# The MLP of a decoder step by one level of Strassen's algorithm, in two phases

## What is computed

```python
def out_and_mlp(x, a, b, w_out, g_mlp, w_up, w_down):
    x = x + jnp.concatenate([a, b], axis=-1) @ w_out
    hn = rmsnorm(x, g_mlp)
    return x + jnp.square(jax.nn.relu(hn @ w_up)) @ w_down
...
    y_prompt = rmsnorm(xp, g_final)
    y_sample = rmsnorm(xs, g_final)
```

## Time and profile before

| | before |
|---|---|
| median of 3 runs (1789.96 to 1799.34) | 1791.36 us |
| span of the profiled execution, first to last instruction | 1663.6 us |
| around the span, against the median | 127.8 us |
| TensorE busy | 1624.7 us, 98% |
| VectorE, ScalarE, GpSimd busy | 52%, 41%, 35% |
| mean granted TensorE clock | 0.987 |
| the MLP, first matmul to the end | 888 to 1664 us |

### The profile page before, as it was taken

One profiled execution on the slowest core, in us unless ns is written; L12 is line 12 of the kernel. 1 busy time (PEld: TensorE's weight loads), 2 busy tenths in 40 slices (PEclk: granted clock), 3 DMA queues, 4 the chain that ended last, 5 costly groups with the idle time before them and its releaser, 6 DMA issues.

```text
span 1663.6 us, 29654 instructions
## 1 busy us (share of the span) xinstructions
PE 1624.7 (98%) x11324; PEld 1395.8 (84%) x11324; DVE 857.5 (52%) x2059; ACT 686.5 (41%) x1448; POOL 587.2 (35%) x715
## 2 busy tenths in 40 slices
PE   8999999999989999999999999999999999999997
PEld 6653464699976777676899999999999999999997
DVE  5486889987644566765545323232323224232424
ACT  4574887688246655553522212122221212222223
POOL 1100333468467777773235031232305022231300
PEclk8999999999989999999999999999999999999999
DMA  8211302235589877779201020111111020111102
GB/s 252 62 51 55 116 28 79 58 90 172 188 262 319 295 248 222 253 207 277 75 1 51 18 85 1 59 43 50 50 50 50 0 101 0 50 50 50 64 2 107
DMA packets 88619, 174.34 MB, mean 105 GB/s; under 512 B 10619, under 2 KB 38639, under 8 KB 88258
## 3 DMA queue, kind: packets, MB, share of 16 engines
q1 hardware_dynamic: 67138, 101.17, 18.4%
q0 software_dynamic: 21376, 71.75, 14.0%
HBM read 152.01 MB, written 20.88 MB: 104 GB/s over the span
## 4 chain that ended last, share of the span: by engine, by line
PE 80%; DVE 7%; issue 6%; DMA 4%; ACT 1%; POOL 1%; SPq 0%; DVEq 0%; ACTq 0%; POOLq 0%
PE psum L2046 8%; PE psum L2044 8%; PE psum L2034 8%; PE psum L2032 8%; PE psum L2033 8%; PE psum L2045 8%; PE psum L1707 3%; PE psum L1827 2%; PE psum L1849 2%; PE psum L1867 2%; PE psum L1506 2%; PE psum L1969 2%; PE psum L1973 2%; PE psum L1968 2%; PE psum L1549 2%
## 5 line engine op out<-in xcount | busy, mean ns | idle before, releaser
L1373 ACT ACTIVATE hrelu<-psum 128x384 f32<-128x384 f32 (+1 forms) x96 | 45.5, 474 | 504.1 <-PE psum L2034 504.1
L2032 PE MATMUL psum<-n_hi,wup_hi 128*128 128x384 f32 (+1 forms) x768 | 251.0, 327 | 0.0
L2044 PE MATMUL psum<-h_hi,wdn_hi 128*128 128x384 f32 (+1 forms) x768 | 250.9, 327 | 0.0
L2034 PE MATMUL psum<-n_hi,wup_lo 128*128 128x384 f32 (+1 forms) x768 | 250.8, 327 | 0.0
L2033 PE MATMUL psum<-n_lo,wup_hi 128*128 128x384 f32 (+1 forms) x768 | 250.8, 327 | 0.0
L2046 PE MATMUL psum<-h_hi,wdn_lo 128*128 128x384 f32 (+1 forms) x768 | 250.2, 326 | 0.0
L2045 PE MATMUL psum<-h_lo,wdn_hi 128*128 128x384 f32 (+1 forms) x768 | 250.0, 326 | 0.0
L2699 DVE TENSOR_TENSOR h_lo<-h_full,h_hi 128x384 fp32r<-128x384 f32 (+1 forms) x96 | 115.7, 1219 | 257.8 <-ACT h_hi L1381 249.0
L2704 DVE TENSOR_TENSOR x_region<-psum,x_region 128x384 f32<-128x384 f32 (+1 forms) x192 | 102.9, 536 | 252.8 <-PE psum L2046 251.7
L1044 POOL TENSOR_TENSOR wup_lo<-wup_full,wup_hi 128x4096 fp32r<-128x4096 f32 x8 | 72.5, 9064 | 384.6 <-ACT wup_hi L1349 384.6
L1220 ACT ACTIVATE arena<-x_region,arena 128x384 bf16<-128x384 f32 (+2 forms) x192 | 166.5, 872 | 6.4 <-POOL arena L969 6.3
(11 more groups left out here) (349 smaller groups left out, 3118.4 us busy)
## 6 DMA issues: line engine op xcount, KB each, us to landing
wup_full<-in_w_up SPq DMA_DIRECT2D x8, 2048.0 KB, 7.7
wdn_full<-in_w_down SPq DMA_DIRECT2D x8, 2048.0 KB, 7.9
arena<-k_scratch SPq DMA_DIRECT2D x32, 256.0 KB
arena<-in_x_prompt SPq DMA_DIRECT2D x14, 512.0 KB, 11.4
arena<-in_w_in SPq DMA_DIRECT2D x3, 2048.0 KB
arena<-in_w_in SPq DMA_DIRECT2D x12, 512.0 KB, 6.0
k_scratch<-arena SPq DMA_DIRECT2D x24, 256.0 KB, 2.6
out<-arena SPq DMA_DIRECT2D x17, 256.0 KB, 3.4
```

The costliest lines, as they stand in the source:

```text
L2032: pe.matmul(b, wu_hi[:, k, col], n_hi[:, k, o:o + w], start=(k == 0), stop=False)
L2034: i = pe.matmul(b, wu_lo[:, k, col], n_hi[:, k, o:o + w], start=False, stop=(k == KT - 1))
L2044: pe.matmul(b, wd_hi[:, f, col], h_hi[:, hf, 0:w], start=(f == 0), stop=False)
```

## The change

The prompt's MLP runs by Strassen's algorithm in Winograd's form: each matrix product is cut in quarters, and seven products of half size stand for eight, with sums before and behind. It has two phases.

Up: 16 groups of 256 hidden features. The activation quarters and their sums (`n`, `xT` used as a buffer, `t4`) are made once, by token blocks of 64 (even and odd blocks are the two halves). Per group SP loads raw w_up (1 MB), GpSimd makes four sums of 512 columns, ScalarE seven high parts, VectorE seven low parts; TensorE runs seven products of 12 matmuls (512 token columns; in group 0 in two passes of 384 and 128). Products 3, 5 and 6 accumulate onto banks that hold 0, 2 and 4. ScalarE and VectorE combine and square them to h, VectorE makes four sums, and SP stores seven tiles of 256 KB to `hscr`. GpSimd also makes the four sums of w_down, through DRAM (`sscr`). x goes to `xscr` before the phase and comes back in the next one.

Down: 112 steps (product i, group k) of 12 matmuls of 512 columns in four banks. Each step's operands (2 x 256 KB) come into a ring of six slots; ScalarE makes the high part (1024 columns), VectorE the low part.

The sample tokens are stationary operands of 64 columns: per up group 48 matmuls with 128 moving columns, in 4 of 7 down products 3 matmuls of 512 a step. The final norm turns all second halves and the sample tile during the last product, and the first halves of the eight prompt tiles behind it.

The diff, cut to its core (i is a product, v a pass, g a group):

```diff
+VG = [(0, 0, 6), (0, 6, 8)] + [(g, 0, 8) for g in range(1, NG)]
+UPBANK = [(0, 1, 2, 0, 3, 2, 3), (4, 5, 6, 4, 1, 6, 1)]
+CHAINED = (3, 5, 6)
+DN_SAMPLE = {0: "h1", 1: "h2", 4: "hd", 5: "h1"}
+RING = 6
+ROWS_EARLY = [(t, 1) for t in range(NB)] + [(NB, 1), (NB, 0)]
...
@@ SP
+            for c in range(3):
+                park(c)
             sp.wait_ge(wo_ready, 3 * KT)
-            sp.dma_start(wd_full, w_dn_v[:, 0:4, :]).then_inc(wdn_in, 16)
...
+            raw_up(1)
+            raw_down(0)
+            sums_down(0)
+            for g in range(NG):
+                v = LASTV[g]
+                if g:
+                    raw_down(g)
+                    h_late(v - 1, g - 1)
+                    if g + 1 < NG:
+                        sp.wait_ge(w_low, 7 * g + 7)
+                        raw_up(g + 1)
+                    sums_down(g)
+                h_early(v, g)
+                if g == NG - 1:
+                    sp.wait_ge(us_done, 2 * NG - 1)
+                    fill(1)
+                    sp.wait_ge(up_done, 7 * LASTV[NG - 1] + 5)
+                    fill(2)
+                h_sums(v, g)
+            sp.wait_ge(us_done, 2 * NG)
+            fill(3)
...
@@ GpSimd
+            for g in range(NG):
+                down_sums(g)
+                if g + 1 < NG:
+                    for x in (1, 2, 3, 4):
+                        up_sum(g + 1, x)
@@ ScalarE
+            squares(0, 0, KT)
+            token_root(0)
+            squares(1, 0, 4)
+            for i in range(7):
+                up_high(0, i)
+            squares(1, 4, 5)
+            norm_high(0)
+            squares(1, 5, KT)
+            token_root(1)
+            squares(2, 0, 3)
+            norm_high(1)
+            squares(2, 3, 4)
+            t4_high(0)
+            t4_high(1)
+            squares(2, 4, KT)
+            token_root(2)
+            norm_high(2)
+            t4_high(2)
...
+            for v, (g, lo, hi) in enumerate(VG):
+                end = v == LASTV[g]
+                if g:
+                    up_high(g, 3)
+                first_product(v)
+                if g:
+                    for i in (4, 5, 6):
+                        up_high(g, i)
+                h_from_bank(v)
+                if end and g + 1 < NG:
+                    up_high(g + 1, 0)
+                    up_high(g + 1, 1)
+                h_from_tile(v, h22, 1)
...
+            for s in range(3, DN_STEPS):
+                dn_high_part(s)
+                if s == 3:
+                    hs_high_part(0, 30)
...
+            for t in range(NB):
+                y_square(len(ROWS_EARLY) + t)
+                y_root(t)
+                act.wait_ge(row_scaled, ROW_SCALED0 + t + 1)
+                act.wait_ge(g_scaled, G_SCALED0 + t + 1)
+                act.activation(yrow[t][:, 512:1024], yrow[t][:, 512:1024], ACT.Copy, scale=yroot[:, t:t + 1]).then_inc(y_rows, 1)
@@ TensorE
-                if u == KT + 3:
+                if u == KT + 1:
                     rms(0)
-                if u == 2 * KT + 3:
+                if u == 2 * KT + 1:
                     rms(1)
...
+            def up_product(v, i):
+                pe.wait_ge(w_low, 7 * g + i + 1)
+                if v == 0:
+                    pe.wait_ge(n_low, {0: 2, 2: 2, 4: 2, 5: 2}.get(i, 4))
...
+                if i == 3:
+                    pe.wait_ge(up_act, v + 1)
+                if i == 5:
+                    pe.wait_ge(up_dve, 5 * v + 2)
+                if i == 6:
+                    pe.wait_ge(up_dve, 5 * v + 3)
+                for k in range(4):
+                    first = k == 0 and i not in CHAINED
+                    pe.matmul(out, wu_hi[i][:, k, :], b_side(i, k, 0, lo, hi), start=first, stop=False, skip_group_check=True)
+                    pe.matmul(out, wu_hi[i][:, k, :], b_side(i, k, 1, lo, hi), start=False, stop=False, skip_group_check=True)
+                    ins = pe.matmul(out, wu_lo[i][:, k, :], b_side(i, k, 0, lo, hi), start=False, stop=(k == 3), skip_group_check=True)
...
+            for v, (g, lo, hi) in enumerate(VG):
+                end = v == LASTV[g]
+                up_product(v, 0)
+                if g:
+                    turn_sample_h(g - 1)
+                up_product(v, 1)
+                if v == 0:
+                    rms(2)
+                up_product(v, 2)
+                if end:
+                    up_sample(g, 0)
+                for i in (3, 4, 5, 6):
+                    up_product(v, i)
+                if end:
+                    up_sample(g, 1)
...
+            def dn_product(s):
+                pe.wait_ge(dn_low, DN_LOW0 + s + 1)
...
+                    if s < NG:
+                        pe.wait_ge(hs_low, HS_LOW0 + (1 if k < 15 else 2))
...
@@ VectorE
                 dve.tensor_tensor(xT[:, j, o:o + w], bank(u % 6)[:, 0:w], xT[:, j, o:o + w], ALU.add).then_inc(wo_done, 1)
+                if u == KT + 1:
+                    norm(0)
                 if u == KT + 4:
-                    rms(0)
+                    low_early(0)
+                if u == KT + 5:
+                    for n in range(7):
+                        up_low(0, n)
+                if u == 2 * KT + 1:
+                    norm(1)
                 if u == 2 * KT + 4:
-                    rms(1)
-            rms(2)
+                    low_early(1)
+                    norm_t4(0)
+                    norm_t4(1)
+                if u == 2 * KT + 5:
+                    low_late(0)
+                    low_late(1)
+            norm(2)
+            norm_t4(2)
+            low_last()
...
+                if g:
+                    up_low(g, 3)
+                if v:
+                    last_h_sum(v - 1)
+                dve.wait_ge(up_act, v + 1)
+                add_bank(v, 0, 1, u, u)
+                if g:
+                    keep_sample_h(g - 1)
+                    for i in (4, 5, 6):
+                        up_low(g, i)
...
+                add_bank(v, 1, 2, h22, u)
+                if end and g + 1 < NG:
+                    up_low(g + 1, 0)
+                add_bank(v, 2, 4, h22, h22)
+                if end and g + 1 < NG:
+                    up_low(g + 1, 1)
+                    up_low(g + 1, 2)
...
+                add_bank(v, 3, 5, h12, u)
...
+                add_bank(v, 4, 6, u, u)
+                dve.wait_ge(h_made, H_MADE0 + 4 * v + 3)
+                h_sum(v, 0, t3_, h22, h12, ALU.subtract)
...
```

More of the change, by code:

```diff
@@ L1070, in _, with squares @@
         def _(act):
-            def rms(c):
+            def squares(c, lo, hi):
                 o, w = CH[c]
-                for k in range(KT):
+                for k in range(lo, hi):
                     n = 8 * c + k
```

801 lines of the change are left out of this document (598 added, 203 removed).

## The result

| | before | changed |
|---|---|---|
| median beside each other, 4 runs of each | 1795.35 us | 1864.82 us (1851.14 to 1874.24) |
| ratio, 95% interval | | 1.040 (1.034 to 1.045) |
| the same on another chip, 9 and 4 runs | 1782.53 | 1853.86; 1.038 (1.035 to 1.041) |
| span of the profiled execution | 1663.6, a second one 1778.8 | 1861.2, a second one 1862.9 |
| mean granted TensorE clock | 0.987 and 0.973 | 0.946 and 0.948 |

A forecast was written before the change was run, and what follows sets the result against it. TensorE was taken to bound the kernel, busy 100 of 100 us in the MLP. Start 21, loop 21, phase change with clock 11.4, end 15, less 30 saved, gave +38.4 on 1791.4: 1830 us, range 1790 to 1862.

The forecast's parts named there:

- TensorE's work: TensorE's matmuls and transposes in the MLP: 736 us against 765.7, so 30 us saved.
- my lower bound of 0.067: Sample tokens' up matmuls of 128 columns: 0.067 us each by the column law; 0.088 was taken, halfway to 0.109.
- Rival 2: Narrow matmuls cost several passes, 128 columns as much as 512 (0.227 us): kernel at 1925 us; chance 0.08.
- rival 4: Matmuls of 512 columns cost 0.213 us, so gain and waits nearly cancel: 1793 us, no change; chance 0.09.
- The start: TensorE's waits from the end of w_out through group 0 of the up phase: 21 us, 15 to 26.
- The loop: Up phase, TensorE's wait before product 6 in each of 14 groups: 1.5 us each, 21 us in all.
- Rival 1: The preparation on ScalarE, VectorE and GpSimd hides after all, from w_out to group 15: 1786 or 1771 us; chance 0.10.
- Rival 3: The raw w_up loads come late, each microsecond costing 14: 1849 or 1892 us; chance 0.12.
- The change of phase: Between up and down, TensorE's wait before the first sample product: 8.4 us, 11.4 with clock allowances.
- The clock: Half granted clock behind idle TensorE: 1.5 us at the change of phase and as much at the start.
- The end: From the last add to the kernel's end, the final norm of eight tiles: 15 us more, 11 to 18.
- The signs: Prediction wrong if an up-phase group takes under 24 us, or three named TensorE waits are under half their forecast.

The follow-up runs named there:

- x4_start: The changed kernel with only the start of the up phase reordered on ScalarE and VectorE, seven low parts of the weights coming later: 1844.72 us, 1.036 of the kernel before.
- x1_lows_first: The changed kernel with VectorE making low parts 4, 5 and 6 ahead of product 1's add, in all groups but the first: 1822.13 us, 1.024 of the kernel before.
- x7_no_sums: The changed kernel with VectorE's up_low(g,0) no longer waiting for GpSimd's two sums, from group 1 on: 1816.20 us, 1.020 of the kernel before.
- x5_all: The changed kernel with four reorderings together (low parts before the first add, change of phase, start, tail): 1794.58 us, 1.006 of the kernel before.
- x6_packed: x5_all plus the edit of x7_no_sums, earlier low parts at the start, and sample tokens' high and low parts packed as one weight: 1783.70 us, 0.993.

## Why the prediction was right or wrong

**TensorE's work: right, by two errors of opposite sign.** 512 columns down cost 0.227, as worked out: six distances in 1.35 us, 0.226 each.

```profile
1700.82 0.39 PE L2433 MATMUL psum<-ring_hi 128*128 128x512 f32 x1
...
1702.18 0.39 PE L2433 MATMUL psum<-ring_hi 128*128 128x512 f32 x1
```

Up they cost 0.234 in six of seven products, 7.6 us more than the sum has (1080 matmuls). The sample products of 128 columns cost 0.060 (16 distances in 0.97 us), not 0.088:

```profile
1183.09 0.22 PE L2377 MATMUL psum<-wu_hi,n_lo 128*64 128x128 f32 x1
...
1184.06 0.44 PE L2356 MATMUL psum<-n_hi,wu_hi 128*128 128x512 f32 x1
```

That is 21 us less, and below my lower bound of 0.067: halfway between two bounds was the wrong choice. The bound from the earlier trace rows didn't apply: its operations have weights of 128 columns and these have 64. With weights of 128 columns the 84 prompt matmuls of 128 columns do cost 0.111 (forecast 0.109). The Trainium skill ("TensorE: Matmul & The Clock Gate", Back-to-back issue gap) gives 81 ns for 128 columns; the trace has 60 with 64-column weights and 111 with 128-column ones, so it agrees with neither. Rival 2 is out, since 128 columns cost far less than 512 (0.060 and 0.111 against 0.227), and so is rival 4, since the 512-column matmuls cost 0.227 to 0.234 and not 0.213.

**The start: places right, one price short.** The waits before products 1, 3, 5 and 6 of group 0 were forecast as 4.7, 12.3 and 1.7 and were 5.2, 11.5 and 2.6. rms(2), forecast as 1 us, didn't wait. rms(1) was forecast as 1.3 and waited 5.4; the w_out stage lost 7.5. The step had counted the squares' sum behind VectorE's seven low parts but with too short a queue; x4_start moved those and got 6.2 back.

**The loop: right in its chain, short by 9 us.** 2.1 us a group instead of 1.5, within its 0 to 4. SP's issue came 1.4 us later into the group than forecast, and GpSimd, which the forecast has busy until the load lands, was idle for 1.7 us before it. Rival 1, that the preparation hides, is out as the kernel stands; x1_lows_first and x7_no_sums show that most of the loop's part hides once one link is moved. Rival 3, late loads, is out too: their median is the forecast's 5.5.

**The change of phase: 14.0 instead of 8.4.** The forecast had one wait, before the sample product, and it was 3 us longer (11.4). There is a second, of 2.6 us, before the fourth bank of the first down step: that bank is released by the add of the last up product, which stands on VectorE behind `dn_low_part(1)`, as the trace shows. The prediction didn't walk through that queue.

**The clock: the step that failed.** It was put at 3 us, 1.5 each at the start and at the change of phase. The row it rested on, showed a half clock behind a stretch in which TensorE was busy for less than a third. The prediction used it for the two long waits only and took the 14 short ones as their own length. The runs showed 65 us at half clock in the MLP and 19.5 us lost in it outside the waits: 16.5 us more than the term has, the largest error of the sum and half of the 33 us by which the stages differ from it. Some 2 us more were lost this way in w_out's stage, behind the wait at rms(1), in the 4.2 us of this row (columns as in the earlier trace rows):

```profile
994.40:998.60 4.20, 4.20 (x13) 3.59 (x14) 0.00 (x0) 0.94 (x2) 0.45 (x1) 0.50 0.75 268
```

x1_lows_first and x7_no_sums confirm it as a consequence of the waits: 23 us fewer of these, and 10 to 13 us of slow matmuls went with them.

**The end: right** (16.3 for 15).

**The range.** It went by rivals and not by terms: the far ends of the start, the loop, the end and TensorE's saving (26, 56, 18 and 13) with the 11.4 of the phase add up to 1890. The measured time went 3 us past the 1862 that I gave, less than its own runs differ. The two terms that I gave no range, the clock and the change of phase, are 22 of the 33 us. The terms weren't independent either: each chain that was longer than I had read it (w_out's stage, the loop, the change of phase, 20 us together) could also bring more half clock.

**The signs.** Neither sign of being wrong that I had named came: the groups take 24.1 to 27.8 us, not under 24, and the three waits are not under half of what I gave. Both look at the waits; neither looks at the clock behind them, which was the error.

## What to carry to other kernels

A wait of TensorE can cost the slow matmuls behind it as well as its length, and waits of 2 us did so too: here 63 us of waits in the MLP brought 20 more, and taking 23 us of them out of the loop gave 10 to 13 besides. The four waits of 1.0 to 1.3 us brought nothing. When a change takes work from the engine that sets the end, read the orders of all the others anew. Here, moving operations on VectorE, ScalarE and SP, with no work removed, was worth 55 us of the MLP (x5_all), and the kernel was still 0.6% behind the one before; it came 1.7% ahead only with the sample tokens packed and six orders more. A chain in series is removed at whichever link is cheapest; look for the wait that protects nothing and for the load whose buffer is freed by the last step of a long list.

## What the runs showed of the hardware that I hadn't expected

- Products 0 to 5 of the up phase take 0.234 us at 512 moving columns where product 6 and the prompt's down products take 0.227 to 0.230, whether the columns are neighbours or pieces of 64. The cause is open.
- A matmul of 128 moving columns takes 0.060 us behind 64-column weights and 0.111 behind 128-column ones; 256 moving columns behind 128-column weights take 0.120 (x6_packed).
- The attention stage took 316 us in one execution of the kernel before and 430 in another, with the same instructions (3684 and 3683 of TensorE), at 259 and 191 GB/s. Two executions of one program can differ by more in a stage that hangs on gathers than a change does elsewhere, so a difference is to be read stage by stage.
